# Two neighbourhood heads as one chain: scores on row halves, values on column halves of one PSUM bank

## Chip, cores and metric

One core of one Trainium2 chip runs the whole program in one launch. The metric is the device time of that launch in microseconds. The engines are named as the profile names them: PE does matmuls (PEld its weight loads), DVE is the vector engine, ACT the activation engine, SP issues the transfers, POOL does nothing here.

## The reference, cut to what matters

Two transformer blocks follow each other, 256 tokens wide and 1024 deep. The first has two layers (recurrent, mLSTM and memory branches, a dense and a mixture feed-forward); the change doesn't touch it. The second block has two layers over x (256 tokens) and a context (256 tokens). Its layer 0 mixes four differential heads with eight neighbourhood heads of width 64. The context's queries see the context's keys alone; the queries of x see the context's 256 keys and those of their grid neighbourhood in x, with a learned bias:

```python
def plain_attention(q, k, v):                    # the context's heads
    s = jnp.einsum('bqhd,bnhd->bhqn', q, k).astype(jnp.float32) * (HEAD_DIM ** -0.5)
    p = jax.nn.softmax(s, axis=-1).astype(v.dtype)
    return jnp.einsum('bhqn,bnhd->bqhd', p, v)

def row_fn(args):                                # the heads of x, one grid row of queries
    ...
    s_nb = jnp.einsum('bchd,bicjhd->bhcij', q_r, k_r).astype(jnp.float32) * scale + bias
    s_ctx = jnp.einsum('bchd,bnhd->bhcn', q_r, kcx).astype(jnp.float32) * scale
    s = jnp.concatenate([s_nb.reshape(B, NA_HEADS, GRID_W, kr * kc), s_ctx], axis=-1)
    p = jax.nn.softmax(s, axis=-1).astype(v.dtype)
    ...
    return (jnp.einsum('bhcij,bicjhd->bchd', p_nb, v_r)
            + jnp.einsum('bhcn,bnhd->bchd', p_ctx, vcx))
```

After the mixer come the output projection and the feed-forward, for x and for the context, each with its own modulation (shift, gain, gate) made from a vector c.

## The kernel before

**Data.** Activations lie transposed, features on the 128 partitions. Large products split both operands into a high and a low f32r part and add three products (L1566 to L1568, or L1517 to L1519 where the weights are stationary); the weights are split on the chip, the high part by ACT (L1899), the low part by DVE (L2299), 1 MB tile by tile, in a ring of three raw tiles and a ring of three split ones. Attention products are exact f32.

**Order.** `Plan` writes one list of units by hand-written rules and a small model of time: `put` adds a unit and moves `clock` on by the unit's PE cost, and `work` gives the costs on ACT and DVE. All four engine programs then walk through the same list, so each engine executes its share strictly in this order, and waits by semaphores. Foreground work is the blocks of a linear stage (`block`), each cut into parts (two parts of 12 matmuls for 256 tokens). After every part `weave` looks at the background chains that are due. A chain (`Chain`) is a generator that puts its next units and yields the clock from which it wants to go on. At most `lanes` chains are live; others wait in `side`. `until` runs chains with no foreground; with `fill` it puts in modulation products (`ada`, L1621, whose weights are loaded from HBM) when no chain is due.

**A head.** `head` makes one chain of one head. For each of the two blocks of 128 queries: unit `s` (the score product, L1648; for the heads of x also a product with the identity that adds the bias tile, L1654), `e` (DVE's row maximum, L2523, and ACT's exponential with row sum, L2036), `n` (DVE's reciprocal L2537 and scaling L2540), `t` (PE transposes L1665, copied by ACT, L2047). Then `v`, the product of the values with the transposed probabilities for both blocks (L1677), copied by ACT (L2053). Head `hd` has its queries and keys on partitions 0-63 or 64-127 as `hd` is even or odd, and its result on the same half. So an even and an odd head of a pair share one block of 128 features. In `roomy` differential heads (part 1) the two members' scores, also one on each half of the partitions, are already put one after the other.

**Part 0** is the context's queries (names n0.0 to n0.7, 256 keys): `near(0)` at the start of the input projections with 4 lanes, `near(1)` at their end; `until` waits for them before the output projection `wab0`. Buffers: 6 for probabilities (`ppc`), 4 for transposed probabilities (`ptc`).

**Part 1** is x's queries (n1.0 to n1.7, 512 keys with bias), behind the four differential heads d1.0 to d1.3, with 2 lanes, 2 buffers of each kind (20 and 21). They run along the context's output projection and its feed-forward `g0c`: three groups of up and down projections, 1024, 1024 and 768 wide. The planner waits for all heads (`heads_done`) after the last group's up projections, ahead of its down projection, which is 8 blocks x 6 x 3 = 144 matmuls. x's output projection `wab1` comes after that.

**Bias.** The bias tile of a head of x (256 KB) lies in one of two places, by the parity of the head. `head` waits in the plan until head `hd - 2` is scored, adds the tile and loads it; on the chip SP waits for that score's semaphore. SP issues all its loads in the order of the tile list, so weight tiles behind a bias tile wait with it.

Of the kernel before, what the change touches and what calls it, by code (L numbers as in the profile page):

```python
# [240 lines left out]
def work(p, unit):  # L241

    kind, *args = unit
    if kind == "tile":
        return ((A, 1.85), (V, 2.21))
    if kind == "lin":
        name, t, i, part, parts, side = args
        if part < parts - 1 or side == 0:
            return ()
        g = p.stage[name]  # L250
        wide = g.n / T
        if g.evac == "f32":
            return ((A, 0.08 + 0.22 * wide),) if i % 2 else ((V, 0.08 + 0.27 * wide),)
        if g.evac == "vdtok":
            return ((A, 0.3),) if i % 2 else ((V, 0.35),)
        if g.evac == "silu":
            return ((A, 0.12 + 0.26 * wide),)
        if g.evac == "silu_tanh":
            return ((A, 0.12 + 0.26 * wide), (V, 0.1 + 0.3 * wide))
        if g.evac == "up":  # L260
            return ((V, 0.1 + 0.3 * wide), (A, 0.05 + 0.27 * wide), (V, 0.08 + 0.27 * wide))
        return AFTER[g.evac]
    if kind in ("e", "n", "t", "v"):
        spec = p.heads[args[0]]
# [8 lines left out]
        return ((A, 0.5 if spec["kind"] == "mem" else 0.3),)  # L273
    if kind == "ml":
# [26 lines left out]
class Plan:  # L301
# [261 lines left out]
    def head(self, name, nk, qbs=2, members=1, bias=False, sub=False, **spec):  # L563
# [70 lines left out]
            self.ready.add(name)  # L634
        self.side.append(Chain(chain()))

    def rope(self, name, **spec):

        self.ropes[name] = spec
# [77 lines left out]
def splits_ahead(units, tiles, tile):  # L717

    at, need, newest, by_s = {}, {}, -1, []
    for pos, (kind, *args) in enumerate(units):  # L720
# [6 lines left out]
        elif kind == "up":  # L727
            at["up", args[3], args[0], args[1], args[2]] = pos
        elif kind == "down":
            at["dn", args[2], args[0], args[1]] = pos  # L730
        elif kind == "s":
            at["s", args[0], args[1], args[2]] = pos
        elif kind == "kout":
            at[tuple(args)] = pos
    for t in tiles:
# [374 lines left out]
def second_order(p):  # L1110
# [394 lines left out]
def tensor_program(nc, T_, pe, plan, mem, v):  # L1505
# [136 lines left out]
    def s(name, qb, m):  # L1642
# [13 lines left out]
            last = T_.matmul(ps[:, 256:512], mem["BAND"][:, 0:128], mem["BAND"][:, 128 + qb * T:128 + qb * T + T], start=False, stop=True)  # L1656
        last.then_inc(*pe.done("ps", "s", name, qb, m))

    def t(name, qb):
        spec = plan.heads[name]  # L1660
        out, probs = bank(("t", name, qb)), v.pp(plan.pp.place["pp", name, qb])
# [188 lines left out]
    def region():  # L1850
# [4 lines left out]
        with pe.eng.If(flag == 1):  # L1855
# [5 lines left out]
            pe.wait_point("region_end", ("act", "dve"))  # L1861
        pe.leave(had)
        plan.swap()
    do = {"lin": lin, "kout": kout, "nsum": nsum, "nsum2": nsum2, "ada": ada, "turned": turned, "s": s, "t": t, "v": vv, "sub1": sub1, "rope1": rope1, "if": iff, "acol": acol,
          "ml": ml, "router": router, "rtop": rtop, "slots": slots, "tt": tt, "gather": gather, "up": up, "turn": turn, "down": down,
          "finish": finish, "region": region}
    for kind, *args in plan.units:
# [13 lines left out]
def scalar_program(nc, S, ac, plan, mem, v):  # L1881
# [168 lines left out]
    def vv(name):  # L2050
        out, src = result_of(v, plan.heads[name], bank(("v", name)))
        ac.wait_ge("ps", "v", name)
        S.activation(out, src, ACT.Copy).then_inc(*ac.done("free_a", "v", name))  # L2053

    def sub0(name):
        spec = plan.heads[name]
        ac.wait_ge("free_a", "v", name)
# [159 lines left out]
    def lam2():  # L2217
# [5 lines left out]
    do = {"start": start, "lam": lam, "tile": tile, "lin": lin, "nsq": nsq, "nmid": nmid, "napp": napp, "cva": cva, "e": e, "t": t, "v": vv, "sub0": sub0, "sub2": sub2, "rgc": rgc, "rowin": rowin, "row": row, "rowout": rowout,  # L2223
          "ml": ml, "pair": pair, "yml": yml, "mga": mga, "h2a": h2a, "adac": adac, "rtop": rtop, "tt": tt, "gather": gather, "up": up, "turn": turn,
          "leave": leave, "region": region, "second": second, "lam2": lam2}
    for kind, *args in plan.units:
# [869 lines left out]
```

## Time and profile before

| | |
|---|---|
| runs shown | 3371.98, 3374.03, 3382.2 us (median 3374.03) |
| profiled execution, first to last instruction | 3378.7 us; its own whole time is not listed apart |
| mean granted TensorE clock | 0.976 of full speed |
| busy: PE, PEld, DVE, ACT | 96%, 88%, 69%, 54% |
| mean DMA rate | 214 GB/s |

The profiled span lies between the second and the third of the runs. PE's busy time counts matmuls whose ends are modelled and which overlap their successors; the distance from one start to the next tells what an instruction costs in a stream. An exact f32 matmul appears as two records, one for each pass; a transpose as one. The column PEclk (or the figure before the DMA share in a table of stretches) is the clock granted to TensorE: 1.00 is 2.4 GHz, and the lower level is half of it.

### The profile page before, as it was taken

What the parts mean: (1) busy time and instruction counts of PE and PEld (TensorE: products, weight loads), DVE (VectorE), ACT (ScalarE), POOL (GpSimd) and SP (SyncE); (2) the same over time, 40 slices, a digit from 0 to 9 for tenths busy, and PEclk for the clock granted to TensorE, in tenths of its full rate; (3) what the DMA queues carried; (4) which work ended last, traced back from release to release, by engine and by line L of the source; (5) the groups of instructions that cost most, each with busy time, mean ns of one, the idle gap of its engine ahead of it and who ended that gap; (6) DMA issues with size and microseconds to landing.
All of it is one profiled execution on the core that took longest, in us unless ns stands there. A gap on an engine that the chain in (4) does not pass through costs nothing.

```text
span 3378.7 us, 56020 instructions
## 1 busy us (share of the span) xinstructions
PE 3229.4 (96%) x24147; PEld 2988.9 (88%) x24147; DVE 2334.0 (69%) x2984; ACT 1831.6 (54%) x2188; POOL 0.2 (0%) x4
## 2 busy tenths in 40 slices
PE   8999999999899899999999999899899999999898
PEld 7998999999889799999999999778687989985698
DVE  6877655577776688888888888755575565556455
ACT  5564544455644477777777777633454444334443
POOL 0000000000000000000000000000000000000000
PEclk9999999999999899999999999999899999998899
DMA  6433565454335699899899899621333466530353
GB/s 255 164 138 125 187 236 193 158 193 159 125 125 188 269 367 363 331 357 357 331 356 356 338 357 354 249 85 63 113 136 127 141 234 251 199 124 13 145 187 118
DMA packets 102812, 723.62 MB, mean 214 GB/s; under 512 B 11424, under 2 KB 13344, under 8 KB 16672
## 3 DMA queue, kind: packets, MB, share of 16 engines
q1 hardware_dynamic: 102560, 719.97, 57.3%
q8 instruction: 194, 3.18, 0.4%
q14 instruction: 58, 0.48, 0.0%
HBM read 718.87 MB, written 1.05 MB: 213 GB/s over the span
## 4 chain that ended last, share of the span: by engine, by line
PE 80%; DVE 10%; ACT 7%; issue 2%; DMA 1%; SPq 0%; DVEq 0%; ACTq 0%
PE PS L1566 14%; PE PS L1568 13%; PE PS L1567 13%; PE PS L1517 6%; PE PS L1519 6%; PE PS L1518 6%; DVE WL L2299 4%; PE PS L1835 3%; PE PS L1836 3%; PE PS L1837 3%; ACT WH L1899 3%; PE PS L1677 2%; PE PS L1648 2%; PE PS L1621 1%; PE PS L1665 1%
## 5 line engine op out<-in xcount | busy, mean ns | idle before, releaser
L2299 DVE TENSOR_TENSOR WL<-RAW,WH 128x2048 fp32r<-128x2048 f32 (+2 forms) x428 | 962.8, 2252 | 548.3 <-ACT WH L1899 543.2
L1899 ACT ACTIVATE WH<-RAW 128x2048 fp32r<-128x2048 f32 (+2 forms) x428 | 803.4, 1880 | 243.1 <-PE PS L1568 182.6
L1566 PE MATMUL PS<-PH,WH 128*128 128x256 f32 x2464 | 705.5, 286 | 22.6 <-ACT F L1981 6.1
L1567 PE MATMUL PS<-PL,WH 128*128 128x256 f32 x2464 | 696.4, 283 | 0.0
L1568 PE MATMUL PS<-PH,WL 128*128 128x256 f32 x2464 | 696.3, 283 | 0.0
L2299 DVE TENSOR_TENSOR WL<-F,WH 128x2048 fp32r<-128x2048 f32 x210 | 480.8, 2290 | 79.8 <-ACT WH L1899 79.1
L1566 PE MATMUL PS<-HPH,WH 128*128 128x256 f32 (+1 forms) x1648 | 493.2, 299 | 17.8 <-ACT WH L1899 8.7
L1566 PEld LDWEIGHTS PS<-PH,WH 128*128 128x128 f32 x2464 | 468.9, 190 | 29.2 <-issue 20.5
L1567 PE MATMUL PS<-HPL,WH 128*128 128x256 f32 (+1 forms) x1648 | 481.2, 292 | 0.0
L1568 PE MATMUL PS<-HPH,WL 128*128 128x256 f32 (+1 forms) x1648 | 480.6, 292 | 0.0
L1567 PEld LDWEIGHTS PS<-PL,WH 128*128 128x128 f32 x2464 | 469.1, 190 | 0.6
L1568 PEld LDWEIGHTS PS<-PH,WL 128*128 128x128 f32 x2464 | 468.7, 190 | 0.0
L1899 ACT ACTIVATE WH<-F 128x2048 fp32r<-128x2048 f32 x210 | 403.7, 1923 | 72.1 <-PE PS L1837 48.2
L1517 PE MATMUL PS<-WH,PH 128*128 128x256 f32 x1456 | 417.4, 287 | 2.0 <-DVE WL L2299 1.1
L1518 PE MATMUL PS<-WL,PH 128*128 128x256 f32 x1456 | 407.4, 280 | 0.0
L1519 PE MATMUL PS<-WH,PL 128*128 128x256 f32 x1344 | 376.9, 280 | 0.0
L1566 PEld LDWEIGHTS PS<-HPH,WH 128*128 128x128 f32 x1648 | 317.7, 193 | 36.4 <-issue 20.3
L1567 PEld LDWEIGHTS PS<-HPL,WH 128*128 128x128 f32 x1648 | 318.1, 193 | 4.3
L1568 PEld LDWEIGHTS PS<-HPH,WL 128*128 128x128 f32 x1648 | 317.7, 193 | 4.5
L1517 PEld LDWEIGHTS PS<-WH,PH 128*128 128x128 f32 x1456 | 275.2, 189 | 5.4 <-ACT WH L1899 1.2
L1518 PEld LDWEIGHTS PS<-WL,PH 128*128 128x128 f32 x1456 | 275.6, 189 | 2.8
L1519 PEld LDWEIGHTS PS<-WH,PL 128*128 128x128 f32 x1344 | 253.9, 189 | 0.0
(394 smaller groups left out, 4972.1 us busy)
## 6 DMA issues: line engine op xcount, KB each, us to landing
F<-in_moe_w SPq DMA_DIRECT2D x210, 1024.0 KB, 5.6
RAW<-in_ffn_w SPq DMA_DIRECT2D x130, 1024.0 KB, 5.0
RAW<-in_moe_w SPq DMA_DIRECT2D x126, 1024.0 KB, 5.2
RAW<-in_w_in SPq DMA_DIRECT2D x64, 1024.0 KB, 5.0
F<-in_ada_w SPq DMA_DIRECT2D x18, 1024.0 KB, 11.3
RAW<-in_w_kv SPq DMA_DIRECT2D x16, 1024.0 KB, 5.0
G<-in_ada_w SPq DMA_DIRECT2D x15, 1024.0 KB, 9.0
RAW<-in_w_in_ab SPq DMA_DIRECT2D x12, 1024.0 KB, 5.0
```

What stands on the lines that cost most here:

```text
L1517: T_.matmul(out, lh, rh, start=i == 0, stop=False)
L1518: T_.matmul(out, lh, rl, start=False, stop=False)
L1519: last = T_.matmul(out, ll, rh, start=False, stop=i == n - 1)
L1566: T_.matmul(out, lh, rh, start=first, stop=False)
L1567: T_.matmul(out, lh, rl, start=False, stop=False)
L1568: last = T_.matmul(out, ll, rh, start=False, stop=end)
L1648: last = T_.matmul(ps, l, r, start=i == 0, stop=i == len(ops) - 1 and not spec["bias"])
L1835: T_.matmul(out, oh[:, c], wh, start=j == 0 and k == 0, stop=False)
L1836: T_.matmul(out, oh[:, c], wl, start=False, stop=False)
L1837: last = T_.matmul(out, ol[:, c], wh, start=False, stop=j == 13 and k == 1)
L1899: S.activation(mem["WH"][:, t.s % NHL, 0:m], v.raws[t.slot][:, 0:m], ACT.Copy).then_inc(*ac.done("w_hi", t.s))
L2299: V.tensor_tensor(mem["WL"][:, t.s % NHL, 0:m], v.raws[t.slot][:, 0:m], mem["WH"][:, t.s % NHL, 0:m].bitcast(F32), sub).then_inc(*dv.done( ...
```

## The change

The neighbourhood heads of both parts are made by a new method `twins(a, b, ...)`, one chain for an even head and the odd one behind it. Per block of queries it puts one unit `s2`: the scores of a and b, into two banks, the one from rows 0-63, the other from rows 64-127, and then both bias products. Units `e`, `n` and `t` stay one for each head, put in pairs. One unit `v2` does the values of both: per block of 128 keys a's product into partitions 0-63 and b's into 64-127 of one bank, which ACT copies in one instruction. The chain takes two probability buffers and two transposed buffers at once (`room`: more than one free), so in part 1 it takes all. The bias tiles of both heads are added and loaded together, after the pair before has been scored. The planner's PE costs change: for two heads of part 1 `s2` counts 2.375 us a block (before 1.59 each), `v2` 1.72 us (before 1.72 each), `t` 0.43 (before 0.86); for part 0 `s2` 0.54 (before 0.53 each). Part 0 has no bias.

```diff
@@ class Plan
+    def twins(self, a, b, nk, bias=False, late=False, **spec):
+
+        for name, hd in ((a, spec["hd"]), (b, spec["hd"] + 1)):
+            self.heads[name] = dict(spec, nk=nk, qbs=2, members=1, bias=bias, sub=False, hd=hd)
+        u, near, pair = 0.43 * nk / 256, spec["kind"] == "near", (a, b)
+
+        def room(rotation, choices):
+            return sum(x not in rotation.held for x in choices) > 1
+
+        def chain():
+            if near and bias:
+                hd = spec["hd"]
+                while hd and f"n1.{hd - 1}" not in self.scored:
+                    yield self.clock + 0.5
+                for x in (hd, hd + 1):
+                    t = self.add_tile(("bias", x), self.io["bias"][x], 1, 512, split=False, slot=10 + x % 2,
...
+                    t.end = ("s", f"n1.{x}", 1, 0)
+                    self.put("loads", ("bias", x))
...
+            for qb in range(2):
+                if qb == 0 and not late:
+                    while not room(self.pt, self.ptc):
+                        yield self.clock + 0.3
+                    for x in pair:
+                        self.pt.take(("pt", x), self.ptc, True)
+                while len(self.banks.held) > 5:
+                    yield self.clock + 0.3
+                free = max([self.bank(("s", x, qb, 0), self.bgc, True) for x in pair])
+                at = self.put("s2", a, b, qb, cost=1.25 * u + (0.25 + 0.4 * near) * 2 * bias, after=free)
...
+                while not room(self.pp, self.ppc):
+                    yield self.clock + 0.3
...
+                    exped[x] = self.freed_at["s", x, qb, 0] = self.put("e", x, qb, 0, after=at)
+                    self.banks.let(("s", x, qb, 0))
+                yield exped[a]
+                for x in pair:
+                    scaled[x] = self.put("n", x, qb, 0, after=exped[x])
+                yield scaled[a]
...
+                for x in pair:
+                    free = self.bank(("t", x, qb), self.bgc)
+                    copied = self.freed_at["t", x, qb] = self.put("t", x, qb, cost=u / 2, after=max(free, scaled[x]))
+                    self.pp.let(("pp", x, qb))
+                yield self.clock
+            yield copied
+            free = self.bank(("v", a), self.bgc)
+            copied = self.freed_at["v", a] = self.put("v2", a, b, cost=2 * u, after=max(free, copied))
...
@@ second_order
     def near(t):
-        for hd in range(4 * t, 4 * t + 4):
-            p.head(f"n0.{hd}", 256, kind="near", part=0, hd=hd)
+        for hd in (4 * t, 4 * t + 2):
+            p.twins(f"n0.{hd}", f"n0.{hd + 1}", 256, kind="near", part=0, hd=hd)
...
-    for hd in range(8):
-        p.head(f"n1.{hd}", 512, bias=True, kind="near", part=1, hd=hd)
+    for hd in range(0, 8, 2):
+        p.twins(f"n1.{hd}", f"n1.{hd + 1}", 512, bias=True, kind="near", part=1, hd=hd)
@@ tensor_program
+    def s2(a, b, qb):
...
+        for name in (a, b):
+            (l, r), = scores_of(v, plan.heads[name], 0, qb)
+            last = T_.matmul(out[name], l, r, start=True, stop=not spec["bias"])
...
+        for name in (a, b):
+            if spec["kind"] == "near":
+                tile = plan.tile["bias", plan.heads[name]["hd"]]
+                pe.wait_ge(f"land{tile.slot}", tile.turn)
+                last = T_.matmul(out[name][:, 256:512], mem["BAND"][:, 0:128].bitcast(F32), tile.raw[:, 0, qb * T:qb * T + T], start=False, stop=True)
...
+            last.then_inc(*pe.done("ps", "s", name, qb, 0))
+
+    def v2(a, b):
+
+        out = bank(("v", a))
+        terms = []
+        for name in (a, b):
+            for qb in range(2):
+                pe.wait_ge("free_a", "t", name, qb)
+            (o, ls), = values_of(v, plan.heads[name], out)
+            terms.append((o, ls, v.pt(plan.pt.place["pt", name])))
+        n = len(terms[0][1])
+        for k in range(n):
+            for o, ls, pt in terms:
+                last = T_.matmul(o, ls[k], pt[:, k, 0:T], start=k == 0, stop=k == n - 1)
...
@@ scalar_program
+    def v2(a, b):
...
+        S.activation(out, bank(("v", a))[:, 0:T], ACT.Copy).then_inc(*ac.done("free_a", "v", a))
```

## Rows read from the trace of the kernel before

**Rows 1.** The page: the span, and section 1's busy time of PE.

```profile
span 3378.7 us, 56020 instructions
...
PE 3229.4 (96%) x24147; PEld 2988.9 (88%) x24147; DVE 2334.0 (69%) x2984; ACT 1831.6 (54%) x2188; POOL 0.2 (0%) x4
```

**Rows 2.** Busy time by stretch: us of it, then each engine, clock, DMA.

```profile
2362.00:2402.80 40.80, 32.05 (x216) 23.15 (x214) 16.34 (x57) 14.77 (x42) 0.00 (x0) 0.75 0.33 129
2502.98:2650.40 147.42, 142.27 (x965) 118.38 (x963) 78.70 (x132) 64.72 (x96) 0.00 (x0) 1.00 0.36 132
2650.40:2708.72 58.32, 58.32 (x493) 58.26 (x493) 34.46 (x46) 25.90 (x35) 0.00 (x0) 1.00 0.44 151
```

**Rows 3.** Timeline of PE: score and bias of head n1.0, first block.

```profile
2506.25 0.28 PE L1568 MATMUL PS<-HPH,WL 128*128 128x256 f32 x1
2506.46 1.12 PE L1648 MATMUL PS<-G 64*128 64x512 f32 x2
2507.51 0.70 PE L1654 MATMUL PS<-BIAS,BAND 128*128 128x256 f32 x2
2507.86 0.47 PE L1566 MATMUL PS<-HPH,WH 128*128 128x256 f32 x1
```

**Rows 4.** Timeline of PE: two half-row scores of a differential head.

```profile
2412.44 1.13 PE L1648 MATMUL PS<-G 64*128 64x512 f32 x4
2413.50 0.66 PE L1665 MATMUL PS<-CST,PQ 128*128 128x128 f32 x4
```

**Rows 5.** Timeline of PE: values of one neighbourhood head, part 1.

```profile
2534.39 1.94 PE L1677 MATMUL PS<-PQ,G 128*64 128x256 f32 x8
2536.26 0.39 PE L1566 MATMUL PS<-HPH,WH 128*128 128x256 f32 x1
```

**Rows 6.** Timeline of PE: values of the first four heads, part 0.

```profile
2261.58 2.00 PE L1677 MATMUL PS<-PQ,G 128*64 128x256 f32 x16
2263.51 0.50 PE L1566 MATMUL PS<-HPH,WH 128*128 128x512 f32 x1
```

**Rows 7.** Timeline of PE: modulation products, 32 columns each.

```profile
13.24 1.07 PE L1621 MATMUL PS<-F,C 128*32 128x256 f32 x16
```

**Rows 8.** Timelines of PE, then ACT: the last four heads of part 0.

```profile
2376.45 1.65 PE L1621 MATMUL PS<-RAW,C 128*32 128x256 f32 x16 [3.96 <-DMA RAW<-in_ada_w]
...
2384.00 2.07 PE L1648 MATMUL PS<-G 64*128 64x256 f32 x6
...
2393.54 1.97 PE L1677 MATMUL PS<-PQ,G 128*64 128x256 f32 x4
...
2396.92 2.10 PE L1677 MATMUL PS<-PQ,G 128*64 128x256 f32 x12
...
2398.20 1.24 ACT L2053 ACTIVATE G<-PS 64x256 f32<-64x256 f32 x3 [0.79 <-PE PS L1677]
```

**Rows 9.** Groups by line, 2502.98 to 2650.4: busy us, mean ns, idle before.

```profile
L2540 DVE TENSOR_SCALAR PQ<-PQ,SM 128x512 f32<-128x512 f32 x16 | 7.8, 487 | 0.6
...
L2053 ACT ACTIVATE G<-PS 64x256 f32<-64x256 f32 x7 | 2.6, 376 | 10.9 <-PE PS L1677 10.9
...
L2537 DVE RECIPROCAL SM<-SM 128x1 f32<-128x1 f32 x16 | 2.5, 155 | 0.0
```

**Rows 10.** Waits of PE in 2502.98 to 2650.4: us, times, longest.

```profile
PE PS L1665 <- DVE PQ L2540: 3.0, 4, 1.3
PE PS L1677 <- ACT PQ L2047: 2.1, 1, 2.1
```

**Rows 11.** Timeline of SP's issues: a bias load and the weights behind.

```profile
2520.55 0.33 SPq L2853 DMA_DIRECT2D BIAS<-in_bias  x1
2520.92 0.43 SPq L2853 DMA_DIRECT2D RAW<-in_ffn_w  x1
```

**Rows 12.** Chain that ended last: first and last DVE or ACT piece between.

```profile
2580.74 0.40 ACT TMP L2007
...
2611.16 0.50 DVE PQ L2540
```

More of the change, by code:

```diff
@@ L273, in work @@
         return ((A, 0.5 if spec["kind"] == "mem" else 0.3),)
+    if kind == "v2":
+        return ((A, 0.4),)
     if kind == "ml":
@@ L635, in head @@
         self.side.append(Chain(chain()))
+    def twins(self, a, b, nk, bias=False, late=False, **spec):
[11 more added lines that the diff above has]
+                    t = self.add_tile(("bias", x), self.io["bias"][x], 1, 512, split=False, slot=10 + x % 2,
+                                      after=() if hd else [("ps", "v", f"d0.{i}") for i in range(4)] + [("ps", "v", f"n0.{i}") for i in range(8)] + [("band_r",)])
+                    t.end = ("s", f"n1.{x}", 1, 0)
+                    self.put("loads", ("bias", x))
+            blocks, turned = head_needs(self.heads[b])
+            blocks, turned = head_needs(self.heads[a])[0] + blocks, head_needs(self.heads[a])[1] + turned
+            ready = max([self.at.get(k, 0.0) for k in blocks] + [self.at.get(("roped", r), 0.0) for r in turned])
+            yield ready
+            copied = 0.0
+            for qb in range(2):
[8 more added lines that the diff above has]
+                at = self.put("s2", a, b, qb, cost=1.25 * u + (0.25 + 0.4 * near) * 2 * bias, after=free)
+                if qb:
+                    self.scored.update(pair)
+                yield at
+                while not room(self.pp, self.ppc):
+                    yield self.clock + 0.3
+                exped, scaled = {}, {}
+                for x in pair:
+                    self.pp.take(("pp", x, qb), self.ppc, True)
+                    self.small[x, qb, 0] = 4 * (self.n["small"] % 32)
+                    self.n["small"] += 1
+                    exped[x] = self.freed_at["s", x, qb, 0] = self.put("e", x, qb, 0, after=at)
[4 more added lines that the diff above has]
+                yield scaled[a]
+                if qb == 0 and late:
+                    while not room(self.pt, self.ptc):
+                        yield self.clock + 0.3
+                    for x in pair:
+                        self.pt.take(("pt", x), self.ptc, True)
+                for x in pair:
+                    free = self.bank(("t", x, qb), self.bgc)
[5 more added lines that the diff above has]
+            copied = self.freed_at["v", a] = self.put("v2", a, b, cost=2 * u, after=max(free, copied))
+            for x in pair:
+                self.pt.let(("pt", x))
+                self.at["head", x] = copied
+                self.ready.add(x)
+        self.side.append(Chain(chain()))
@@ L1657, in s @@
         last.then_inc(*pe.done("ps", "s", name, qb, m))
+    def s2(a, b, qb):
+        out = {}
+        for name in (a, b):
+            spec = plan.heads[name]
+            head_ready(spec)
+            out[name] = bank(("s", name, qb, 0))[:, 0:spec["nk"]]
+        for name in (a, b):
+            (l, r), = scores_of(v, plan.heads[name], 0, qb)
+            last = T_.matmul(out[name], l, r, start=True, stop=not spec["bias"])
+            if not spec["bias"]:
+                last.then_inc(*pe.done("ps", "s", name, qb, 0))
+        if not spec["bias"]:
+            return
+        pe.wait_ge("band_r")
+        for name in (a, b):
[3 more added lines that the diff above has]
+                last = T_.matmul(out[name][:, 256:512], mem["BAND"][:, 0:128].bitcast(F32), tile.raw[:, 0, qb * T:qb * T + T], start=False, stop=True)
+            else:
+                c = 128 - 128 * qb
+                last = T_.matmul(out[name][:, 256 + c:384 + c], mem["BAND"][:, 0:128], mem["BAND"][:, 128 + qb * T + c:256 + qb * T + c], start=False, stop=True)
+            last.then_inc(*pe.done("ps", "s", name, qb, 0))
+    def v2(a, b):
+        out = bank(("v", a))
+        terms = []
+        for name in (a, b):
+            for qb in range(2):
[6 more added lines that the diff above has]
+                last = T_.matmul(o, ls[k], pt[:, k, 0:T], start=k == 0, stop=k == n - 1)
+        last.then_inc(*pe.done("ps", "v", a))
+        pe.also("ps", "v", b)
+        for name in (a, b):
+            pe.frees("pt", name)
     def t(name, qb):
@@ L2053, in vv @@
         S.activation(out, src, ACT.Copy).then_inc(*ac.done("free_a", "v", name))
+    def v2(a, b):
+        spec = plan.heads[a]
+        q0 = spec["part"] * T if spec["kind"] == "near" else 0
+        out = buf["G1" if spec["kind"] == "near" else "Q8"][:, spec["hd"] // 2, q0:q0 + T]
+        ac.wait_ge("ps", "v", b)
+        S.activation(out, bank(("v", a))[:, 0:T], ACT.Copy).then_inc(*ac.done("free_a", "v", a))
+        ac.also("free_a", "v", b)
     def sub0(name):
@@ L2222, in lam2 @@
         S.activation(mem["LVS"][:, 2:4], mem["LVS"][:, 0:2], ACT.Exp).then_inc(*ac.done("lam2_e"))
-    do = {"start": start, "lam": lam, "tile": tile, "lin": lin, "nsq": nsq, "nmid": nmid, "napp": napp, "cva": cva, "e": e, "t": t, "v": vv, "sub0": sub0, "sub2": sub2, "rgc": rgc, "rowin": rowin, "row": row, "rowout": rowout,
+    do = {"start": start, "lam": lam, "tile": tile, "lin": lin, "nsq": nsq, "nmid": nmid, "napp": napp, "cva": cva, "e": e, "t": t, "v": vv, "v2": v2, "sub0": sub0, "sub2": sub2, "rgc": rgc, "rowin": rowin, "row": row, "rowout": rowout,
           "ml": ml, "pair": pair, "yml": yml, "mga": mga, "h2a": h2a, "adac": adac, "rtop": rtop, "tt": tt, "gather": gather, "up": up, "turn": turn,
```

4 lines of the change are left out of this document (3 added, 1 removed).

## Prediction

> **What bounds the kernel now.** I read the page first. PE, the matmul engine, is busy 96% of the span, DVE 69%, ACT 54% [rows 1], so time is saved where PE is given less to do, and only in stretches where PE is the one that is full. The neighbourhood heads lie in two places, so the second view is the table of busy time by stretch [rows 2]. In the first place (part 0, the context's queries, 2362 to 2402.8 us at its end) PE is busy 32.05 of 40.80 us at a mean granted clock of 0.75: a stretch of latencies. In the second (part 1, the eight heads of x, 2502.98 to 2650.4) PE is busy 142.27 of 147.42 us, DVE 78.70, ACT 64.72, at the full clock. These heads are threaded into the context's feed-forward matmuls, and each pair of them takes 147.42 / 4 = 36.9 us. So part 1 is PE's, and 5.15 us of it is idle by the table. From the last head to 2708.72 PE is busy 58.32 of 58.32 us with nothing of the heads: head results are late to nobody there. Third, I read PE's timeline around single instructions, for their start-to-start times; a matmul's own length overlaps the next one and must not be added up. An exact-f32 matmul leaves two records (two passes).
>
> **Part 1, scores.** Now each head and query block issues one 64-row by 512-column product (2 records) and one bias product. From the first score record to the first bias record it takes 2507.51 - 2506.46 = 1.05 us, and from there to the next feed-forward matmul 0.35 [rows 3]. The change issues two heads' scores next to each other on row halves 0-63 and 64-127, then both bias products on all rows. What two such scores cost side by side the trace shows already, since the differential heads of part 1 are issued so: 4 records, from 2412.44 to the next instruction at 2413.50, 1.06 us [rows 4]. Four records in the time of two: the second head's score is free, 1.05 us saved for each pair and block. The change also enters and leaves the half-row shape once instead of twice: the start before a score is 0.21 us after its predecessor against 0.12 between feed-forward matmuls, and the matmul after the bias lasts 0.47 against 0.28 [rows 3]. That is 0.09 + 0.19, taken as 0.25. With 4 pairs x 2 blocks: 8 x (1.05 + 0.25) = 10.4 us.
>
> The four records of [rows 4] fill two slots of 0.53 us, though the program orders them a1, a2, b1, b2: b's first pass doesn't wait for a's second. The Trainium skill ("TensorE: Matmul & The Clock Gate", Part 3) says that matmuls keep program order, with only weight loads pulled ahead; by that a pair would fill three slots (a1; a2 with b1; b2). Row and rule differ, and the sum stays with the row.
>
> **Part 1, values.** One head is 4 key blocks x 2 passes = 8 records, from 2534.39 to 2536.26, 1.87 us, with the following matmul 0.39 long instead of 0.28 and the same 0.09 at the entry [rows 5]: 2.07 us. The change issues a and b alternately per key block, on output partitions 0-63 and 64-127 of one bank. In part 0 the lanes happen to put four heads' values together today: 16 records from 2261.58 to 2263.51, 1.93 us [rows 6], where one after another they would take 16 x 1.87 / 8 = 3.74. That they will share a bank is no obstacle: the modulation products put four column groups into one bank, 16 records in 1.07 us [rows 7]. So one head's values disappear per pair: 4 x 2.07 = 8.3 us. PE's removed work in part 1: 10.4 + 8.3 = 18.7 us.
>
> **Part 1, what is added.** (a) The planner puts a's and b's transposes next to each other. b's scaled probabilities come one reciprocal (0.155) and one scale (0.487) after a's on DVE [rows 9], 0.64 us; a's four transposes last about 0.44, so 0.2 us of waiting, 8 times: 1.6 us. If the planner comes late, none. (b) One evacuation of 128x256 on ACT replaces two of 64x256 at 0.376 [rows 9]: 4 x 0.38 less on ACT, covered by PE today and worth nothing by itself. (c) Softmax work on DVE and ACT is unchanged, only bunched; so are transposes and their copies. (d) The eight bias loads come two at a time. SP issues in order, and a bias load waits until the tile's previous head has been scored, with the feed-forward weights queued behind it: today it sits so until 2520.55, and the weights behind it leave at 2520.92 [rows 11]. With the change three such waits remain, for two loads each. I cost it at nothing: the waiting time per two heads is the same, but it does not shrink either.
> (e) The important one: PE's idle 5.15 us will not stay. Of it 3.0 us was for probabilities and 2.1 for a copied transpose [rows 10]. Between 2580.74 and 2611.66 the chain that ended last runs through 31 us of ACT, DVE and issue alone, splits of weights and softmax steps behind each other in their queues [rows 12], while PE was kept busy. A pair's 36.9 us less PE's 18.7 / 4 = 4.7 is 32.2 us, barely above such a chain. So PE will meet these queues more often. Below: the old idle time goes too (-5 us, since there are fewer places to wait). Above: each of the eight transpose places waits like today's longest, 1.3 us [rows 10], 10 us in all, +5 over today's. I take +3: the chain almost fills the shorter stretch.
>
> **Part 0.** Its first four heads already overlap [rows 6], so nothing there. Of the last four, the second block's scores are now one single, then a pair and a single (6 records at 2384.00) and the values 4 and 12 records (2393.54 and 2396.92) in a stretch whose mean granted clock is 0.75 [rows 2, 8]. As pairs the scores save one of the three places there, half of the 2.07 us of the six records, 1.0 us, and ACT's three copies in a row before the last conversion (1.24 us) become one, 0.8 less; some of it lies beside waits. I take 1.5 us. Below: this stretch also carries modulation products that wait 3.96 us for a load [rows 8]; a planner that slips one in or out moves it by that much, so -4 to +5 us.
>
> **Sum.** 18.7 + 1.5 - 1.6 - 3 = 15.6 us less. The profiled execution's span is 3378.7 us, so its span after would be 3363.1. Nothing gives its own whole time; the three runs are 3371.98, 3374.03 and 3382.2, so the span fits between the upper two. Against the median of 3374.03 the prediction is 3358.4, said as 3358.
>
> **Rivals.**
> *Saved work becomes waiting.* As (e), but fully: the ACT and DVE queues, or the weight loads behind the bias loads, set the pace of part 1, and the time stays within 10 us. For: the 31 us chain [rows 12]; against: ACT and DVE together are busy 143 of 147 us only if they never overlapped, and they do [rows 2]. Time: 10 of the 18.7 or more given back, about 3367, up to 3374. Chance 0.17.
> *Slower: the pairs run one after another.* A pair takes both probability buffers and both transposed buffers of part 1 (there are two of each), so a second pair can't start before the first one's values. Today two heads overlap. If a pair needs as long as today's two, 36.9 us, nothing happens. A single head goes from score 2506.5 to values 2534.4, 28 us; two of these in series would be 56 us, 224 for four pairs against 147 now. The results are first needed where the planner waits for the heads, just ahead of that projection: PE has 58.32 us of other work [rows 2], 493 matmuls at 0.118 us, of which the last 144 (17 us, the context's third down projection) come after that point; 41 us are left. The point from which it decides is 36.9 + 41 / 4 = 47 us for a pair. At 56 us the kernel loses 224 - 147 - 41 = 36 us of waiting, less 15.6: 3394. Against: both heads of a pair go through each step together, so the latency should be one head's plus about 2 us a block, 32 us. Chance 0.05; another 0.03 for a planner's reordering in part 0 that costs more than it saves.
> *Less overlap than in the rows.* If b's first pass starts beside a's second, a pair's scores take three slots of 0.53 us [rows 4] and not two: 8 x 0.53 = 4.2 us less gained, 3362.6. For it speaks that a bias product follows here and none there; against it the two slots of every such group of rows. It would still be a gain. Chance 0.08. (The order of matmuls on the page of the Trainium skill named above would lead here; the trace disagrees.)
> *All of it.* Idle time goes as well: 18.7 + 1.5 + 5 = 25, 3349. Chance 0.10.
> *My forecast*, 3352 to 3364: 0.57.
>
> **Numbers.** 0.3% is 10 us, about what a measurement of this kernel can tell from no change; the runs shown spread by 10 themselves. Faster by more than that (below 3364): forecast, all of it, and most of the third rival, 0.74. Same: 0.18. Slower: 0.08. The range, 3348 to 3370, leaves out the slower rival, half of the "becomes waiting" one and the tail of the best case.
>
> **What would show it.** Score groups of part 1 as 4 records in about 1.06 us followed by 4 bias records; values as 16 records in about 1.9 us; 4 value groups instead of 8. The whole of part 1's heads near 132 us instead of 147.42, PE's idle time in it 6 to 10 us. ACT's value copies of neighbourhood heads halved and 128 wide. After the last head still 40 us or more of uninterrupted feed-forward before the projection; a wait of PE just ahead of it would prove the slower rival. The prediction is wrong if PE's waits for probabilities and copies in part 1 sum to over 15 us, if DVE's splits come late, or if the low-clock stretches around part 0 and the differential heads (2362 to 2503) move by several us.

## The result, and the profile after

The changed kernel takes 3385.11 us (median of 16 runs, 3376.7 to 3387.88) against 3372.95 for the kernel before (16 runs, 3367.34 to 3382.2). The ratio is 1.0028, 95% interval 1.002 to 1.0037: 0.28% or 12.2 us slower, where 0.5% faster was forecast. The profiled execution took 3386.72 us, 1.8 more than its span.

The page of the changed kernel, its span and section 1 (busy us, share, instructions), against [rows 1]:

```profile
span 3384.9 us, 56012 instructions
...
PE 3214.6 (95%) x24147; PEld 2983.7 (88%) x24147; DVE 2333.9 (69%) x2984; ACT 1829.0 (54%) x2180; POOL 0.2 (0%) x4
```

PE has 14.8 us less to do than in [rows 1], and the span of the profiled execution is 6.2 us longer. So PE waits more. The table of stretches of the changed kernel (us, then PE, PEld, DVE, ACT and POOL busy, clock, DMA share, GB/s) says where, against [rows 2]:

```profile
2502.00:2660.00 158.00, 126.38 (x936) 115.25 (x935) 77.24 (x128) 62.60 (x89) 0.00 (x0) 0.89 0.34 123
2660.00:2720.00 60.00, 60.00 (x507) 59.05 (x506) 35.01 (x48) 25.98 (x35) 0.00 (x0) 1.00 0.48 165
2362.00:2403.00 41.00, 32.83 (x232) 23.61 (x231) 19.37 (x65) 15.65 (x45) 0.00 (x0) 0.79 0.33 129
```

Part 1's stretch has become longer although PE has less to do in it: 159.7 us from the first score (2503.25) to the end of the last values (2662.9), against 144.0 before. 31.6 us of the 158 in the table are idle, where 5.15 of 147.42 were, and the clock fell to 0.89 from 1.00. Part 0 is as it was, and from 2660 on, with the last pair's values, PE is full again.

The timeline of PE in the changed kernel (start, us, line) holds the pair's scores with their biases, and the pair's values, against [rows 3] and [rows 5]:

```profile
2503.25 1.13 PE L1741 MATMUL PS<-G 64*128 64x512 f32 x4
2504.31 0.70 PE L1751 MATMUL PS<-BIAS,BAND 128*128 128x256 f32 x2
2504.85 0.59 PE L1751 MATMUL PS<-PQ,BAND 128*128 128x256 f32 x2
2505.09 0.47 PE L1639 MATMUL PS<-HPH,WH 128*128 128x256 f32 x1
...
2541.94 1.95 PE L1769 MATMUL PS<-PQ,G 128*64 128x256 f32 x16
2543.82 1.13 PE L1741 MATMUL PS<-G 64*128 64x512 f32 x4
```

Two scores take 2504.31 - 2503.25 = 1.06 us, as one did; two heads' values take 1.88 us, as one head's did. What the change is meant to do, it does.

The waits of PE in the changed kernel, 2490 to 2665 (us in total, times, longest), against [rows 10]:

```profile
PE PS L1639 <- issue: 31.1, 3, 11.1
PE PS L1639 <- DVE HPL L2598: 0.5, 1, 0.5
```

No wait for probabilities and none for a copied transpose is left. In their place stand three waits of a plain feed-forward matmul (L1639) that the profile can put down to no releaser ("issue"). All three lie the same way. The first of them, in the timelines of the changed kernel: PE, then ACT, then DVE:

```profile
2519.77 1.13 PE L1741 MATMUL PS<-G 64*128 64x512 f32 x4
...
2524.51 0.27 PE L1641 MATMUL PS<-HPH,WL 128*128 128x256 f32 x1
2534.51 0.55 PE L1639 MATMUL PS<-HPH,WH 128*128 128x256 f32 x1 [9.72 <-issue]
...
2523.85 0.19 ACT L2152 ACTIVATION_READ_ACCUMULATOR PQ<-PS,SM 128x1 f32 x1
2530.17 1.91 ACT L2015 ACTIVATE WH<-RAW 128x2048 fp32r<-128x2048 f32 x1 [6.13 <-DMA RAW<-in_ffn_w]
...
2532.11 2.29 DVE L2424 TENSOR_TENSOR WL<-RAW,WH 128x2048 fp32r<-128x2048 f32 x1 [5.62 <-ACT WH L2015]
```

PE's last matmul before the gap starts 4.7 us after the last score of the first pair, and PE starts again 0.1 us after DVE has made the low part of a weight tile (2532.11 + 2.29 = 2534.40); DVE waited for ACT's high part, and ACT waited 6.13 us for the raw tile from HBM. The reader should not stop at the word "issue": the queue to look at is the one that feeds ACT. The timeline of SP's issues in the changed kernel, the first two places (the third is alike, bias loads at 2603.56 and three weight tiles at 2604.40), against [rows 11]:

```profile
2521.56 0.33 SPq L2978 DMA_DIRECT2D BIAS<-in_bias  x1
2521.99 0.37 SPq L2978 DMA_DIRECT2D PQ<-in_bias  x1
2522.41 1.38 SPq L2978 DMA_DIRECT2D RAW<-in_ffn_w  x3
...
2559.95 0.33 SPq L2978 DMA_DIRECT2D BIAS<-in_bias  x1
2560.38 0.37 SPq L2978 DMA_DIRECT2D PQ<-in_bias  x1
2560.80 12.32 SPq L2978 DMA_DIRECT2D RAW<-in_ffn_w  x4
```

Three weight tiles leave within 1.38 us of each other, right behind the two bias loads, and these leave only when the pair's last score (2519.77 to 2521.6) is done. The three tiles had nothing to wait for but the bias loads ahead of them: the whole ring of raw tiles was empty. Three times PE runs dry until the first of them has landed and is split. A last table of stretches of the changed kernel: the three idle times (10.0, 11.4 and 10.6 us; the first and the sum), then PE's first 4.6, 3.7 and 5.4 us after them (the first and the third):

```profile
2524.52:2534.51 9.99, 0.27 (x4) 0.10 (x2) 3.89 (x6) 3.76 (x2) 0.00 (x0) 0.72 0.81 306
...
sum 31.96, PE 0.82 PEld 0.31 DVE 12.33 ACT 15.15 POOL 0.00; mean PE 0.27 PEld 0.10 DVE 4.11 ACT 5.05 POOL 0.00
...
2534.50:2539.10 4.60, 4.59 (x21) 4.60 (x22) 4.30 (x2) 2.58 (x3) 0.00 (x0) 0.50 0.02 4
...
2615.70:2621.10 5.40, 5.40 (x25) 5.40 (x26) 4.58 (x2) 1.97 (x2) 0.00 (x0) 0.51 0.82 299
```

The idle times sum to 31.96 us from start to start, of which PE waited for 31.1 (the view of waits above). After each the granted clock is 0.50, the lower level, for 13.7 us in all. Matmuls then start 0.213 us apart instead of 0.118, so of these 13.7 us 13.7 x (1 - 0.118 / 0.213) = 6.1 are lost too. Together 37.2 us. Against them stand the 18.7 us of work that the prediction takes from PE and the 5.1 us of old waits that are gone: 13.4 us are left over, and 12.2 were measured.

**Theory.** The change moved the bias tiles forward in the list. In the kernel before, the two lanes are taken by heads hd-2 and hd-1, so the chain of head hd starts, and adds its bias tile, only when hd-2 has put its values: n1.0's values are at 2534.39 [rows 5], its last score 14 us earlier. By then weight tiles for that much PE time stand in the list ahead of the bias tile. In the changed kernel the second lane holds the next pair, whose chain is alive during the pair before it and adds its bias tiles in the very step in which the last score of that pair is put. The list distance between a score and the loads that wait for it went from 14 us of PE time to nothing. The lists that the two planners write can be counted: before, one to three weight tiles are added between a head's last score and the bias tile that waits for it; after, none, at all three places. **Rivals:** the pairs' bunched softmax on ACT and DVE delays the splits (step (e) of the prediction), or the pairs as such (a pair takes all buffers), or part 0.

### The profile page after: what moved, and what is told of

Same layout as the page of the kernel before. It is cut to its first block, busy times and chain, and to the rows that moved or that the text cites. A ratio compares the mean times of both kernels' runs of the same rounds, so it can differ in the third digit from the quotient of the medians.

```text
span 3384.9 us, 56012 instructions
## 1 busy us (share of the span) xinstructions
PE 3214.6 (95%) x24147; PEld 2983.7 (88%) x24147; DVE 2333.9 (69%) x2984; ACT 1829.0 (54%) x2180; POOL 0.2 (0%) x4
## 4 chain that ended last, share of the span: by engine, by line
PE 81%; DVE 9%; ACT 6%; issue 2%; DMA 1%; SPq 0%; DVEq 0%; ACTq 0%
PE PS L1639 14%; PE PS L1640 14%; PE PS L1641 14%; PE PS L1590 6%; PE PS L1592 6%; PE PS L1591 6%; DVE WL L2424 3%; PE PS L1951 3%; PE PS L1952 3%; PE PS L1953 3%; ACT WH L2015 3%; PE PS L1793 2%; PE PS L1721 2%; PE PS L1694 1%; PE PS L1781 1%
## 5 line engine op out<-in xcount | busy, mean ns | idle before, releaser
L1639 PE MATMUL PS<-PH,WH 128*128 128x256 f32 x2464 | 704.7, 286 | 21.5 <-ACT F L2097 6.1
L1639 PE MATMUL PS<-HPH,WH 128*128 128x256 f32 (+1 forms) x1648 | 491.7, 298 | 48.2 <-issue 31.5
L1639 PEld LDWEIGHTS PS<-PH,WH 128*128 128x128 f32 x2464 | 467.7, 190 | 28.6 <-issue 21.0
L1639 PEld LDWEIGHTS PS<-HPH,WH 128*128 128x128 f32 x1648 | 317.9, 193 | 66.4 <-issue 49.3
```

Source lines behind the costliest of these rows:

```text
L1639: T_.matmul(out, lh, rh, start=first, stop=False)
```

## The experiments

Each was timed in five rounds against the kernel before, whose medians in the three groups of runs were 3375.29, 3374.55 and 3376.87 us. The first group holds experiments 1, 3, 4 and 5, the second 2, 6, 8 and 9, the third 7 and 10, so a difference of medians across groups, and against the changed kernel's 3385.11 (3372.95 for the kernel before beside it), carries up to some 4 us of the groups' own. Unless said otherwise an experiment is the changed kernel with the edit shown. In the texts that were set down ahead of the runs, e1 is experiment 1 and e9 experiment 6.

**1. Four places for bias tiles.** Two more places in a buffer that is free then; no load of a pair waits for the score of the pair just before it.

```diff
-  ... slot=10 + x % 2,
-  after=() if hd else ...
+  ... slot=10 + x % 2 if hd % 4 == 0 else 20 + x % 2,
+  after=[("sub_y", f"d1.{i}") for i in range(4)] if hd == 2 else () if hd else ...
...
+    v.raws += [mem["TMP2"][:, i, :] for i in range(2)]
```

> The changed kernel with four places for bias tiles instead of two: pairs 1 and 3 load into two rows of the temporary buffer that the differential heads no longer use, so a pair's bias loads wait for the pair before last, and never for the score that stands just ahead of them. Theory A (the two bias loads stand in SP's list right behind the score that they wait for, and hold the feed-forward weights back): the three idle times of PE, 10.0, 11.4 and 10.6 us from start to start, go, and with them the low granted clock behind them (about 6 us); some of the 5 us of ordinary waits of the kernel before returns. 3385.1 - 32 - 6 + 3 = 3350 us. Rival B (one pair at a time, since a pair takes all the buffers, leaves PE without work): three idle times stay, 3385 us. Rival C (scores and values don't run side by side): refuted already if B and A differ only in waits; its time would be 3369 or more.

Measured: 3351.74 us (3345.9 to 3354.87), ratio 0.9932 [0.9919, 0.9946]. The table of part 1's stretch, PE's waits in it, and SP's issues, of this kernel:

```profile
2498.00:2650.00 152.00, 150.51 (x1190) 138.60 (x1189) 91.58 (x147) 75.10 (x104) 0.00 (x0) 1.00 0.45 159
...
PE PS L1782 <- DVE PQ L2666: 0.7, 1, 0.7
PE PS L1640 <- DVE HPL L2599: 0.5, 1, 0.5
PE PS L1770 <- ACT PQ L2164: 0.3, 2, 0.2
...
2503.91 1.72 SPq L2979 DMA_DIRECT2D TMP<-in_bias  x2
2505.68 1.38 SPq L2979 DMA_DIRECT2D RAW<-in_ffn_w  x3
2520.43 0.33 SPq L2979 DMA_DIRECT2D BIAS<-in_bias  x1
2520.87 0.37 SPq L2979 DMA_DIRECT2D PQ<-in_bias  x1
2521.28 20.53 SPq L2979 DMA_DIRECT2D RAW<-in_ffn_w  x4
```

The three idle times are gone, the clock is 1.00 throughout, and 33 us came back (32 by the ratios). Bias loads still wait for a score at 2520.43, but now for a pair whose successor's bias is already there, and the four weight tiles behind them leave over the next 20.53 us without any matmul waiting for one. The softmax of pairs is as bunched as in the changed kernel, and PE waits 0.7 us for it: that rival falls, and so does the one of the pairs as such.

**2. The same places with single heads** (the kernel before, with four bias places in turn). It separates what the places give by themselves.

> The kernel before (single heads) with four places for bias tiles: how much of the gain of four places was to be had without pairing. Theory A: the kernel before idles 5.15 us in part 1, about 4 of it behind late splits that follow a blocked weight load; 3375 - 4 = 3371 us, so the rest of the 23 us by which four places with pairs beat the kernel before (3351.7 against 3375.3) is pairing. Rival F (the bias loads held back the kernel before as much as the changed one): 3352 to 3356 us.

Measured: 3370.84 us, ratio 0.9989 [0.998, 0.9998]. The places alone give 3.7 us. So pairs against singles with equal places are 3370.84 - 3351.74 = 19.1 us.

**3. Bias tiles early with single heads** (the kernel before). The mechanism without any pair: the tile of head hd + 2 is added in the step that puts hd's last score.

```diff
-                while hd > 1 and f"n1.{hd - 2}" not in self.scored:
-                    yield self.clock + 0.5
...
                             self.scored.add(name)
+                            if spec["kind"] == "near" and bias and spec["hd"] < 6:
+                                bias_tile(spec["hd"] + 2)
```

> The mirror, on the kernel before: heads stay single, nothing is paired, but each head's bias tile is added to SP's list in the step that puts the score it waits for (head hd's last score adds the tile of head hd + 2). Theory A: PE gets idle times of several us behind last scores without any pairing, 3 to 6 of them; 3373 + 15 to 35 = 3388 to 3408 us. Rival B (it is the pairing of buffers that costs): 3373 us, no change.

Measured: 3421.63 us, ratio 1.0142 [1.0126, 1.0158], 13.6 us beyond the expected range on the slow side. PE's waits, 2490 to 2690, in this kernel:

```profile
PE PS L1570 <- issue: 32.5, 4, 9.9
PE PS L1570 <- ACT WH L1903: 5.2, 1, 5.2
```

The same picture in a kernel without pairs (SP issues three weight tiles within 1.38 us from 2583.73, right behind a bias load): the position in the list is enough to make it. More heads mean more of such waits (five of 5.45 to 10.24 us from start to start, 39 in all). Behind them PE works at a granted clock of 0.50 for 26.15 us, which by the reckoning above loses 11.7. The range had left this out: 37.7 us of waits and 11.7, less the 5.1 of [rows 10], are 44.3 of the 46.3 us measured.

**4. Bias tiles added when the pair before is through**, by waiting for transposed buffers instead of for the score.

```diff
-                while hd and f"n1.{hd - 1}" not in self.scored:
+                while hd and not room(self.pt, self.ptc):
```

> The changed kernel with one condition moved: the two bias tiles are added to SP's list when the pair before has given back its buffers (after its values), not when it has been scored. Two places as in the change. Theory A: SP reaches the bias loads while the weights of the next blocks already stand ahead of them in its list, so PE's three idle times of 10 to 11 us go; the bias has been scored for long when the plan reaches it. 3350 us, at most 3 x 3 us more for the bias tile's own landing ahead of the next score: 3350 to 3359. Rival B: 3385, nothing changes, since the pairs still run one after another.

Measured: 3373.49 us, ratio 0.9994 [0.9985, 1.0003]: a miss. 12 us came back, not 30. Two waits of PE are left, of 5.9 and 8.9 us. ACT and then DVE around the second, in this kernel:

```profile
2561.18 1.91 ACT L2015 ACTIVATE WH<-RAW 128x2048 fp32r<-128x2048 f32 x1 [9.37 <-DMA RAW<-in_ffn_w]
...
2563.12 2.29 DVE L2424 TENSOR_TENSOR WL<-RAW,WH 128x2048 fp32r<-128x2048 f32 x1 [10.01 <-ACT WH L2015]
2565.33 0.68 DVE L2648 TENSOR_REDUCE SM<-PS 128x1 f32<-128x512 f32 x1
```

The late weight tile now holds up ACT and DVE while PE still has weights; the next pair's row maximum stands behind the split in DVE's queue, and PE waits for the probabilities. The tile was late since its load left at 2555.15, again behind the two bias loads (2554.30). This edit moves the stall to other victims. The planner's list says why the later position isn't late enough: between a pair's last score and the two bias tiles that wait for it stand one weight tile at the first place, two at the second and three at the third, and the two stalls are at the first two. That a third tile would have spared them too was not tried.

**5. The pairs of part 0 alone**, with single heads in part 1.

> The change in part 0 alone (the context's heads in pairs), the heads of x as in the kernel before. The prediction had 1.5 us of gain for part 0, with -4 to +5 around it; the two traces stand 2.6 us closer at the end of part 0 than at its start. Theory A: 3373 - 1.5 to 3 = 3370 to 3371.5 us, not to be told from no change. Rival D (part 0's new order is what costs): 3380 us or more.

Measured: 3373.21 us, ratio 0.9995 [0.9987, 1.0004], 1.7 us less by the ratio (from 4.4 less to 1.4 more): no part of the loss.

**6. Bias loads issued by POOL.** SP's queue then holds weights only, and nothing of them stands behind a wait for a score.

```diff
@@ sync_program
-            load(plan.tiles[state["sent"]])
+            if plan.tiles[state["sent"]].key[0] != "bias":
+                load(plan.tiles[state["sent"]])
...
@@ pool_program
+            if t.before is not None:
+                po.wait_ge("ps", *t.before.end)
...
+            G_.dma_start(v.raws[t.slot][:, 0:t.kb * t.nc], t.src).then_inc(*po.done(f"land{t.slot}", t.turn, by=16))
```

> The changed kernel with its two places and its order of units, and only the issuer of the bias tiles moved: POOL, which does nothing else, waits for the scores and issues the eight bias loads, so SP's list has feed-forward weights alone. Theory A (what costs is the weight loads queued behind SP's wait, not the wait itself): the three idle times of 10 to 11 us go, as with four places: 3350 us, up to 3356 if POOL's issue is slow enough for a score to wait for its bias. Rival E (the bias tile's own landing, or the buffers, made PE wait): the idle times stay, 3385 us.

Measured: 3371.0 us, ratio 0.9991 [0.9982, 1.0]: a miss by 15 us and more. SP's issues in this kernel, then PE's waits:

```profile
2463.59 155.00 SPq L2978 DMA_DIRECT2D RAW<-in_ffn_w  x19
...
PE PS L1639 <- ACT WH L2015: 15.0, 2, 7.5
PE PS L1639 <- issue: 4.0, 1, 4.0
```

SP is free, yet three waits remain at the same places, 19 us instead of 31. Now they are put down to ACT's split, and ACT was not waiting for data: at the first of them it starts its split at 2526.41, right behind the softmax of the pair. The plan has a second user of the list's order. `splits_ahead` places the splits of a weight tile in ACT's and DVE's queues, and a guard in it lets no tile be split ahead of the latest point that any tile before it in the list waits for, bias tiles included. So weight tiles behind a bias tile are also *split* after the score.

**7. As 6, with the guard passing over bias tiles.**

```diff
-        if t.before is not None:
+        if t.before is not None and t.key[0] != "bias":
```

> As e9 (the changed kernel with its bias loads issued by POOL, so that SP's queue holds weights only), and in addition the planner's guard for splits passes over bias tiles: a weight tile that stands behind a bias tile in the list may now be split as early as its ring allows. Theory A (e9 kept its three waits because the guard still put ACT's and DVE's splits behind the score that the bias tile waits for): the waits of 4.29, 7.76 and 7.76 us before L1639 go, the stretch of x's heads is full on PE as in e1, and the time is that of e1, 3351.7 on the same footing, ratio 0.993 (3347 to 3356). Theory B (e9's waits came from the latency of a pair's chain or from the weights' own transfers, which no list order sets): waits of 4 us and more stay before L1639 or move to the pairs' transposes, and the time stays at e9's 3371.

Measured: 3351.37 us (3343.11 to 3354.34), ratio 0.992 [0.9906, 0.9934]. Part 1's stretch in the table of this kernel:

```profile
2498.00:2650.00 152.00, 151.20 (x1200) 139.69 (x1200) 92.71 (x147) 73.50 (x103) 3.19 (x6) 1.00 0.42 149
```

The same time as with four places, with only two places: what the two ways share is that no weight tile is held back, in SP's queue or in the splits, until the score just put is done. The loss has two parts, SP's queue and the guard of the splits; freeing the first alone gives back 14 us (experiment 6), both 34, by the medians (12 and 36 by the ratios). The guard alone wasn't tried: while SP issues the bias loads, a split placed ahead of the score can wait for a weight tile that SP holds behind a load that waits for that same score, and then each waits for the other. That is what the guard is for.

**8. Scores one after the other** (experiment 1's kernel; score a, bias a, score b, bias b).

```diff
-        for name in (a, b):
-            (l, r), = scores_of(v, plan.heads[name], 0, qb)
-            last = T_.matmul(out[name], l, r, start=True, stop=not spec["bias"])
...
         for name in (a, b):
+            (l, r), = scores_of(v, plan.heads[name], 0, qb)
+            T_.matmul(out[name], l, r, start=True, stop=False)
             if spec["kind"] == "near":
...
```

> On top of the four places: s2 issues score a, bias a, score b, bias b, so the two scores never stand side by side; all else as it is. By the prediction's terms PE gets 8 x (1.05 + 0.25) = 10.4 us more in part 1: 3351.7 + 10.4 = 3362 us, if PE is what bounds it. If the ACT and DVE queues bound part 1 by now, less, 3353 to 3358.

Measured: 3359.26 us, ratio 0.9957 [0.9943, 0.997]: 7.5 us more than experiment 1 by the medians. Its timeline of PE, one pair and block:

```profile
2519.84 1.12 PE L1748 MATMUL PS<-G 64*128 64x512 f32 x2
2520.89 0.70 PE L1752 MATMUL PS<-BIAS,BAND 128*128 128x256 f32 x2
2521.52 1.12 PE L1748 MATMUL PS<-G 64*128 64x512 f32 x2
2522.57 0.70 PE L1752 MATMUL PS<-PQ,BAND 128*128 128x256 f32 x2
2522.92 0.47 PE L1640 MATMUL PS<-HPH,WH 128*128 128x256 f32 x1
```

3.08 us from the first score to the feed-forward, against 2505.09 - 2503.25 = 1.84 side by side: 1.24 for each of eight places, 9.9 us; the prediction had 1.30 and 10.4.

**9. Values one after the other** (experiment 1's kernel; all four key blocks of a, then those of b).

```diff
-        for k in range(n):
-            for o, ls, pt in terms:
+        for o, ls, pt in terms:
+            for k in range(n):
```

> On top of the four places: v2 issues all four key blocks of a and then all four of b, instead of alternating. Reading of the rows of before (column halves run as two streams, each in its own order, and b needn't wait for a): 16 records still take about 1.9 us, 3351.7 us, no change. Rival (strict program order of matmuls): the values of a pair take 3.7 us, 4 x 1.8 = 7 us more in part 1 and less in part 0: 3359 to 3361 us.

Measured: 3352.95 us, ratio 0.9938, 1.2 us more than experiment 1 by the medians, which five runs of each don't separate. The trace separates them. PE's timeline, the first pair's values of this kernel:

```profile
2529.30 2.86 PE L1770 MATMUL PS<-PQ,G 128*64 128x256 f32 x16
2532.09 1.13 PE L1742 MATMUL PS<-G 64*128 64x512 f32 x4
```

2.79 us, where alternating order takes 1.88 and strict turns would take 3.74. Unmerged, the 16 records start at 0, 0.27, 0.48, 0.70, 0.91, 0.92, 1.13, 1.19, 1.35, 1.40, 1.56, 1.62, 1.83, 2.05, 2.27 and 2.48 us: b's first key block goes beside a's third, ahead of a's fourth. So the column half of b is used before a has been issued in full, but not from the start. (Which record is whose is read from the lengths and spacings: two series 0.22 us apart, each opened by a record of 0.43 us, the second 0.92 us behind the first.) Neither expectation held: the values are not free of the order, and not strictly in it. The order of the two loops is worth 0.91 x 4 = 3.6 us of PE time.

**10. The sixteen window heads of the next layer in pairs too**, on top of experiment 1.

```diff
-        for hd in range(4 * t, 4 * t + 4):
-            p.head(f"c.{hd}", 512, bias=True, kind="swa", hd=hd)
+        for hd in range(4 * t, 4 * t + 4, 2):
+            p.twins(f"c.{hd}", f"c.{hd + 1}", 512, bias=True, kind="swa", hd=hd)
```

> e1 with the sixteen window heads of the layer behind (names c.0 to c.15, 512 keys with bias, 64-wide) put in pairs too; they are issued single in every kernel so far. Their rows in e1: a score 1.05 us (two records), values of one head 1.73 to 1.87 us (8 records), and PE busy 153.76 of 165.00 us in their stretch (2965 to 3130). If PE sets the pace there, each pair saves 2 x 1.05 + 1.85 + some 0.5 for entering the narrow shapes less often, 4.45 us, times 8 pairs 35.6 us at most. The stretch already has 11.2 us of idle time, and its matmul work lies between dependent steps (query norms and rope), so a part is lost to latency: expected 20 us less than e1, 3332 (3322 to 3342). Rival (latency sets the pace, the pair's chain is as long as two singles in turn): saved work becomes waiting, no more than 5 us less than e1, 3347 to 3357, with PE's waits for PQ or G grown by 20 us and more.

Measured: 3320.33 us (3319.64 to 3325.78), ratio 0.9832 [0.9819, 0.9846]; 31.4 us less than experiment 1 by the medians, above the 20 expected, 1.7 us outside the range on the fast side, and near the bound of 35.6 for a stretch in which PE sets the pace. This is the fastest version: 1.68% faster than the kernel before. These heads' biases come from no load of their own, so nothing stands behind them.

## Why the prediction was wrong

**The step that failed is (d)**: "With the change three such waits remain, for two loads each. I cost it at nothing: the waiting time per two heads is the same, but it does not shrink either". The count was right, and the length nearly. These are SP's waits for the scores' last products, 2440 to 2660, before and after (us, times, longest):

```profile
SPq L2853 <- PE PS L1654: 84.8, 6, 23.8
...
SPq L2978 <- PE PS L1751: 99.8, 3, 36.1
```

For two heads that is 28 us before and 33 after. The error is to read the cost off the length of the wait. What decides is what has been issued ahead of the wait. The change moved the bias tiles in the list from 14 us behind the score to right at it, so the ring of weights was empty when the wait ended. It cost 31.1 us of waiting PE and 6.1 us of half clock, and removing it gave 33 (experiments 1 and 7). Experiment 3 shows it without pairs. The remaining 4 us between 37 and 33 weren't settled. About 1 of them is ordinary waits that come back in experiment 1, and the mean granted clock of the changed kernel's 16 runs alone lies between 0.972 and 0.978.

The rows shown for this step held the warning: [rows 11] has weights leaving 0.37 us behind a bias load. The prediction took from it that the wait exists today, and not how PE survives it, namely by weights loaded earlier. The diff had the rest: `while hd and ... not in self.scored` asks for the score alone, and the two lanes hold two pairs instead of two heads. The first rival did name "the weight loads behind the bias loads", but bounded the loss by the gain (3374) as if the stall could only eat what PE had saved.

**Scores**, forecast 10.4 us: measured 1.06 us for two, and 9.9 by the timeline of experiment 8 (7.5 by its medians). The rival of less overlap (three slots) fell with it. **Values**, 8.3: 1.88 us for two heads' instead of 3.74, which is 7.4 for four pairs without the narrow shape's entries. The Trainium skill ("TensorE: Matmul & The Clock Gate", Part 3) says that matmuls start in program order; experiment 9's records don't agree: b's first starts before a's fourth key block, which is ahead of it in the program.

**Terms (a) and (e)**, forecast 1.6 and 3 us of new waiting: experiment 1, where (d) is out of the way, has 0.7 and 0.3 us of such waits in place of the 5.1 of [rows 10]. PE is busy 150.51 of 152 us, at 60% DVE and 49% ACT. The 31 us chain of [rows 12] didn't bind. Together: pairs against singles with equal places are 19.1 us (experiments 1 and 2), of which 1.7 belong to part 0; 17.4 for part 1, against 18.7 of removed work and the 14.1 that the sum kept. By these medians the terms were mis-sized by some 3 us, on the cautious side; part 0's share is uncertain by as much.

**Part 0**, forecast 1.5: measured 1.7 by the ratio (experiment 5), within its interval of 4.4 less to 1.4 more.

**The slower rival** (pairs one after another) did not occur: PE has 60.00 of 60.00 us of work after the heads. The kernel is slower by another mechanism. The prediction's sum closes once (d) has its price: 3358.4 + 37.2, less the 4.6 of terms (a) and (e) and the 5.1 of old waits, none of which the changed kernel shows, is 3385.9, and 3385.11 was measured (the baseline of the sum, 3374.03, is 1.1 us above the median of 16 runs). Without the fault of (d) the change gives 3351.74, near the "all of it" case of 3349.

## What to carry to other kernels

Where one queue issues loads in order and one of them waits for a computation, the cost of the wait is not its length but how much of what stands behind it is needed before it ends; so for each such load find what is ahead of it in the list, before and after the change. A change that merges two work items also changes when their preparations are put, since the number of items alive stays and their size doubles. And when a list serves several users (here the loads' order and the place of the splits), freeing one of them gives back only its part: 14 of 34 us here.

## What the runs showed of the hardware

Matmuls on separate column halves overlap even where the program has them some instructions apart, but only over a short distance: two key blocks apart they ran side by side, four apart they did not at first (2.79 us for 16 records instead of 1.88). After 10 to 11.4 us without a matmul TensorE's clock was granted at its lower level for the first 3.7 to 5.4 us of new work, 6.1 us lost in three places, a fifth on top of the idle time itself.
